# The second layer's normalised rows: scaled by ScalarE and VectorE and turned plainly, in place of products with a diagonal

## What is computed

```python
def second_block(x, ...):
    h = rms_norm(x, norm_mix_pre)
    u = h @ w_in                       # queries, keys, values, gates, convolution parts
    ... attention and a short convolution give y ...
    x = x + rms_norm(y @ w_out, norm_mix_post)
    h = rms_norm(x, norm_ffn_pre)
    gu = causal_dwconv(h @ w_ffn_up, ffn_conv_w)
    g, up = split(gu)
    y = (gelu(g) * up) @ w_ffn_down
    return x + rms_norm(y, norm_ffn_post)
```

## Time and profile before

| | |
|---|---|
| median of 3 runs | 1407.34 us (1405.52 to 1411.5) |
| the profiled execution | 1411.11 us, span 1409.3 us |
| granted TensorE clock, mean | 0.984 of full |
| TensorE busy | 1335.4 us (95% of the span) |
| VectorE busy | 757.2 us (54%) |
| ScalarE busy | 579.9 us (41%) |
| GpSimd busy | 456.9 us (32%) |
| chain that ended last | TensorE 76%, VectorE 15%, ScalarE 3% |

### The profile page before, as it was taken

One profiled execution on the slowest core, in us unless ns is written; L12 is line 12 of the kernel. 1 busy time (PEld: TensorE's weight loads), 2 busy tenths in 40 slices (PEclk: granted clock), 3 DMA queues, 4 the chain that ended last, 5 costly groups with the idle time before them and its releaser, 6 DMA issues.

```text
span 1409.3 us, 22598 instructions
## 1 busy us (share of the span) xinstructions
PE 1335.4 (95%) x9338; PEld 1111.0 (79%) x9338; DVE 757.2 (54%) x1246; ACT 579.9 (41%) x879; POOL 456.9 (32%) x131
## 2 busy tenths in 40 slices
PE   4999888889999999999999999999999999999998
PEld 3778677777788888888888787777798888888886
DVE  7788688664765444354327538787265444443002
ACT  7535465253442223221126545655265334433212
POOL 4424243033214434444422320000213433443344
PEclk8999899998999999999999999999999999999999
DMA  9564400302323333223313511101212232223211
GB/s 377 219 235 165 149 3 2 122 25 69 101 79 120 125 145 120 90 90 125 114 63 104 230 61 34 58 31 61 105 60 90 93 115 92 90 90 126 98 60 60
DMA packets 25901, 147.92 MB, mean 105 GB/s; under 512 B 2849, under 2 KB 4001, under 8 KB 11209
## 3 DMA queue, kind: packets, MB, share of 16 engines
q1 hardware_dynamic: 22272, 134.21, 26.6%
q10 hardware_dynamic: 3528, 12.28, 2.3%
HBM read 144.36 MB, written 4.74 MB: 106 GB/s over the span
## 4 chain that ended last, share of the span: by engine, by line
PE 76%; DVE 15%; ACT 3%; issue 2%; DMA 2%; POOL 1%; SPq 0%; DVEq 0%; ACTq 0%; POOLq 0%
PE bank L2198 22%; PE bank L2199 21%; PE bank L2200 21%; PE bank L2466 4%; DMA raw<-in_weights 2%; DVE xres L1760 1%; DVE raw L1812 1%; PE bank L1204 1%; ACT weight_hi L1409 1%; PE bank L1197 1%; DVE xres L1763 1%; PE bank L1188 1%; POOL weight_lo L1355 1%; POOL xres L1390 1%; DVE bank L1756 1%
## 5 line engine op out<-in xcount | busy, mean ns | idle before, releaser
L1355 POOL TENSOR_TENSOR weight_lo<-raw,weight_hi 128x2048 fp32r<-128x2048 f32 (+2 forms) x84 | 388.9, 4630 | 816.4 <-ACT weight_hi L1409 816.4
L2198 PE MATMUL bank<-act_hi,weight_hi 128*128 128x512 f32 (+1 forms) x1136 | 435.6, 383 | 18.3 <-DVE act_lo L1760 10.0
L2199 PE MATMUL bank<-act_lo,weight_hi 128*128 128x512 f32 (+1 forms) x1136 | 424.8, 374 | 0.0
L2200 PE MATMUL bank<-act_hi,weight_lo 128*128 128x512 f32 (+1 forms) x1136 | 424.7, 374 | 0.0
L1409 ACT ACTIVATE weight_hi<-raw 128x2048 fp32r<-128x2048 f32 (+1 forms) x98 | 185.3, 1891 | 428.9 <-PE bank L2200 394.7
L2198 PEld LDWEIGHTS bank<-act_hi,weight_hi 128*128 128x128 f32 x1136 | 215.2, 189 | 66.6 <-issue 18.3
L2200 PEld LDWEIGHTS bank<-act_hi,weight_lo 128*128 128x128 f32 x1136 | 215.1, 189 | 38.8
L2199 PEld LDWEIGHTS bank<-act_lo,weight_hi 128*128 128x128 f32 x1136 | 215.4, 190 | 34.6 <-issue 0.2
L2198 PE MATMUL bank<-weight_hi,hid_hi 128*128 128x512 f32 x352 | 136.9, 389 | 0.0
L2199 PE MATMUL bank<-weight_lo,hid_hi 128*128 128x512 f32 x352 | 136.9, 389 | 0.0
L2200 PE MATMUL bank<-weight_hi,hid_lo 128*128 128x512 f32 x352 | 136.9, 389 | 0.0
(11 more groups left out here) (385 smaller groups left out, 1826.2 us busy)
## 6 DMA issues: line engine op xcount, KB each, us to landing
raw<-in_weights SPq DMA_DIRECT2D x112, 1024.0 KB, 4.8
first_piece<-in_first_ada SPq DMA_DIRECT2D x15, 512.0 KB, 15.8
w<-in_w ACTq DMA_DIRECT2D x2, 2048.0 KB, 12.0
bias_rows<-bias_rows_once ACTq DMA_DIRECT2D x1, 2560.0 KB
xres<-in_x SPq DMA_DIRECT2D x4, 512.0 KB, 5.6
strip<-bias_rows ACTq DMA_DIRECT2D x1, 2048.0 KB, 8.3
out<-xres SPq DMA_DIRECT2D x3, 512.0 KB, 2.6
row_a<-in_ln_g ACTq DMA_DIRECT2D x2, 512.0 KB, 4.1
```

The costliest lines, as they stand in the source:

```text
L1355: pool.tensor_tensor(wlo[i % SPLIT][:, :size], raw[n % RAW][:, :size], whi[i % SPLIT][:, :size], ALU.subtract).then_inc(lo_ready, 1)
L2198: pe.matmul(o, l[0], r[0], start=first, stop=False)
L2199: pe.matmul(o, l[0], r[1], start=False, stop=False)
L2200: return pe.matmul(o, l[1], r[0], start=False, stop=last)
```

## The change

The diagonal and its tile are gone. The row itself is scaled into `xn2`, and `turn_half` turns it with `pe.transpose` as in the first layer. ScalarE scales rows 0 and 2 whole (1024 wide) and the second half of row 3, and in h4 that of row 1; VectorE, behind its reciprocal in `inverse_x`, scales the first half of row 3, in h4 the first half of row 1, and in h3 both halves of row 1, each 512 wide. Two semaphores, `rows_act` and `rows_vector`, take the place of `xn3_ready`, and `turn_half` waits for a row's parts where their blocks begin (`scaled_rows_of`). In h4, row 0 is turned before the k = 0 step of the last row of `out2_3` and row 1 between it and the k = 1 step; and row 0 is scaled ahead of the conversion and not behind it.

```diff
-    diag, _ = place("diag", [P, TT, P], F32, arena + 6 * TT * DM)

...
- ... "ss3", "root3", "xn3_ready", "grow_ready", ...
+ ... "ss3", "root3", "rows_act", "rows_vector", "grow_ready", ...
...
@@ -714,6 +713,12 @@
     row2_a, a2 = place("row2_a", [P, DM], F32, e1 - FT * SEQ * 4)
     row2_b, a2 = place("row2_b", [P, DM], F32, a2)
 
+
+    def scaled_rows_of(e):
+
+        act, vector = S["rows_act"], S["rows_vector"]
+        return ([[(act, 1)], [(vector, 1), (vector, 2)], [(act, 2)], [(vector, 3), (act, 3)]],
+                [[(act, 4)], [(vector, 4), (act, 5)], [(act, 6)], [(vector, 5), (act, 7)]])[e]
 
     def second_act(act, a, convert, affine_half, square_x, root_x, scaled_x):
         act.wait_ge(load["strip0"], 16)
@@ -848,9 +853,9 @@
                 squares_of_rows("mix2", 0, x, rms_t)
             square_x(1, t)
             root_x(1, t)
+            scaled_x(1, t)
             if half == 0:
                 convert()
-            scaled_x(1, t)
             square_x(1, u)
             root_x(1, u)
             scaled_x(1, u)
@@ -1152,7 +1157,7 @@
                 mm = pe.transpose(bank(("turn_v", name))[:, n * t:n * t + n], before_turn[name][0:n, tok(t)], ident[0:n, 0:n])
             fill(("turn_v", name), mm)
 
-        dense_halves(FIRST_UNITS[:2], "h3", xres, (S["xn3_ready"], 0))
+        dense_halves(FIRST_UNITS[:2], "h3", xn2, scaled_rows_of(0))
         for n, name in enumerate(FIRST_UNITS):
             if name == "gates":
                 gates_features()
@@ -1232,8 +1237,8 @@
         dense_rows("mix2", "out2", 4, [(act_hi, act_lo)] * 2 + [(out_hi, out_lo)] * 2,
                    ready={0: (S["y2_lo"], 2), 1: (S["y2_lo"], 4), 2: drained_at(("values", PAIR_END[1]), "dve"),
                           3: drained_at(("values", PAIR_END[3]), "dve")}, turned=True,
-                   turn=("h4", xres, (S["xn3_ready"], TT)))
-        dense_halves(("up2_0", "up2_1"), "h4", xres, (S["xn3_ready"], TT))
+                   turn=("h4", xn2, scaled_rows_of(1)))
+        dense_halves(("up2_0", "up2_1"), "h4", xn2, scaled_rows_of(1))
         for m in range(2, FT):
             dense_feature(f"up2_{m}", 2)
         dense_rows("ff2", "down2", FT // 2, [(hid_hi, hid_lo)] * (FT // 2),
@@ -1728,8 +1733,9 @@
 
         def scaled_x(e, t):
 
+            h = slice(SEQ * (t % 2), DM)
             act.wait_ge(S["x_inverse"], TT * e + t + 1)
-            a.done(act.activation(diag[:, t, :], ident[:], ACT.Copy, scale=x_sums[:, t:t + 1]), S["xn3_ready"])
+            a.done(act.activation(xn2[:, t, h], xres[:, t, h], ACT.Copy, scale=x_sums[:, t:t + 1]), S["rows_act"])
 
         for half in range(2):
             t, u = 2 * half, 2 * half + 1
@@ -1740,7 +1746,8 @@
             for x in (t, u):
                 square_x(0, x)
                 root_x(0, x)
-                scaled_x(0, x)
+                if x != 1:
+                    scaled_x(0, x)
             if half == 0:
                 convert()
             affine_half("h3", half, "nmp")
@@ -2100,6 +2107,9 @@
         def inverse_x(e, t):
             dve.wait_ge(S["x_rms_root"], TT * e + t + 1)
             d.step(V.reciprocal(x_sums[:, t:t + 1], x_sums[:, t:t + 1]), S["x_inverse"])
+            for j in range(2 if (e, t) == (0, 1) else t % 2):
+                h = slice(SEQ * j, SEQ * j + SEQ)
+                ts(xn2[:, t, h], xres[:, t, h], x_sums[:, t:t + 1], sem=S["rows_vector"])
 
         def affine_lo_half(stage, half, part):
 
@@ -2296,26 +2306,28 @@
                     if ready is not None and n in ready:
                         pe.wait_ge(*ready[n])
                 for t in tiles:
-                    if turn is not None and (n, t) == (n_units - 1, TT - 1):
-                        turn_half(turn[0], 0, *turn[1:])
                     for k in range(2):
+                        if turn is not None and (n, t) == (n_units - 1, TT - 1):
+                            if turn[0] == "h4":
+                                turn_half(turn[0], 0, *turn[1:], rows=(k,))
+                            elif k == 0:
+                                turn_half(turn[0], 0, *turn[1:])
                         mm = rows_product(stage, n, n_units, last_two[n], parts, t, k, turned)
                 if tiles == middle and n == n_units - 2:
                     mm.then_inc(unit_used, 1)
 
-        def turn_half(stage, half, source, ready):
-
-            for i in range(KC // 2):
-                claim(pe, (stage, half, i))
-            for t in range(2):
-                pe.wait_ge(ready[0], ready[1] + 2 * half + t + 1)
+        def turn_half(stage, half, source, ready, rows=(0, 1)):
+
+            for t in rows:
+                if t == 0:
+                    for i in range(KC // 2):
+                        claim(pe, (stage, half, i))
+                parts = ready[2 * half + t]
                 for k in range(KC):
+                    if k % (KC // len(parts)) == 0:
+                        pe.wait_ge(*parts[k * len(parts) // KC])
                     at, x = HALF * (k % 2) + P * t, source[:, 2 * half + t, P * k:P * k + P]
-                    o = bank((stage, half, k // 2))[:, at:at + P]
-                    if stage == "h2":
-                        mm = pe.transpose(o, x, ident[:])
-                    else:
-                        mm = pe.matmul(o, x, diag[:, 2 * half + t, :], start=True, stop=True)
+                    mm = pe.transpose(bank((stage, half, k // 2))[:, at:at + P], x, ident[:])
                     if t and k % 2:
                         fill((stage, half, k // 2), mm)
 
@@ -2676,8 +2688,8 @@
                 out1(*args)
 
         dense_rows("mix1", "out1", 4, [(act_hi, act_lo)] * 4, begun, {2: (S["y_lo"], 2), 3: (S["y_lo_last"], 2)},
-                   turn=("h2", xres, (S["xn_ready"], TT)))
-        dense_halves(("up1_0", "up1_1"), "h2", xres, (S["xn_ready"], TT))
+                   turn=("h2", xres, [[(S["xn_ready"], TT + t + 1)] for t in range(TT)]))
+        dense_halves(("up1_0", "up1_1"), "h2", xres, [[(S["xn_ready"], TT + t + 1)] for t in range(TT)])
         for m in range(2, FT):
             dense_feature(f"up1_{m}", 2)
             if m == GATE_ROWS_AT:
```

More of the change, by code:

```diff
@@ L640, in build @@
                              "y_hi", "y_lo_first", "y_lo", "y_lo_last", "gates_ready", "var1", "root1", "xn2_ready", "affine2", "hid_hi_ready",
-                             "hid_ready", "var2", "root2", "offset_ready", "ss3", "root3", "xn3_ready", "grow_ready", "strip_ready", "blk_ready", "hc_ready", "low_ready",
+                             "hid_ready", "var2", "root2", "offset_ready", "ss3", "root3", "rows_act", "rows_vector", "grow_ready", "strip_ready", "blk_ready", "hc_ready", "low_ready",
                              "zeroed", "cmp_scaled", "exp_done", "gate_ready", "o_ready", "upper_free", "y2_hi", "y2_lo", "squares_ready",
```

## The result

The changed kernel takes 1411.58 us against 1408.44 us before, medians of 20 runs each; the ratio is 1.0025 with a 95% interval of 1.0015 to 1.0035, so 3.5 us (2.1 to 4.9) slower; the medians themselves differ by 3.1 us. The forecast was 2.0 us slower and 1409.3 us. Of the 2.3 us by which the time lies over that, 1.1 come from its base, the median of three runs (1407.34) in place of twenty, and the rest from the change.

What follows compares the result with a forecast made beforehand. TensorE was taken as full nearly everywhere, with VectorE late in h3 and h4's second half. Losses of 0.9 us in h3 and 1.1 in h4 sum to 2.0 on 1407.34, giving 1409.3 us; range 1405.3 to 1413.5.

Steps and rivals of the forecast that it cites:

- TensorE's saving: Plain turns in h3 and h4 save TensorE 7.7 us over eight rows, most of it hidden behind waits.
- rival C: h4's VectorE multiplication is not held by GpSimd: h4 1.1 us shorter, kernel 1407.1 us; chance 0.12.
- VectorE's multiplications in h3: Two for row 1 delay h3's first product by 1.04 us; h3 loses 0.9 us in all.
- The side sum with 1.03 us for one multiplication: Upper bound per multiplication: h3 loses 1.3 us, h4 is 0.8 us worse, kernel 1411.4 us.
- The multiplication held by GpSimd: In h4's first half, row 1's multiplication waits for GpSimd's split, ending 2.9 us later than its work needs.
- The claim of up2_0's banks: In h4, up2_0 waits for four low parts: it starts 1.6 us later, or 0.7 earlier without GpSimd.
- The chain through ScalarE's conversion to row 3: In h4's second half, the late conversion shifts VectorE up to row 3's reciprocal by 1.25 us; first product +1.1 us.
- rival B: TensorE's clock falls in the new gaps of h3 and h4: all together 4.3 us, 1413.6 us; chance 0.15.
- the first layer's row: Evidence against a clock fall: in the first layer's second half, turns with 1.6 us idle kept the clock at 1.00.
- the fall at 988 us: Evidence for a clock fall: after thin work the clock stood at 0.50, then 0.69, a loss of 1.6 us.
- D: TensorE's time counts everywhere in h3 and h4: 7.7 us saved, 1399.6 us; chance 0.03.
- E: GpSimd also holds h3's multiplications, costing up to 4.6 us more, 1413.9 us; chance 0.05.

Runs made afterwards that it cites:

- best, first form: Changed kernel with h3's rows 0 and 1 back to the diagonal and h4's row 1 scaled wholly by ScalarE; ratio to the kernel before 1.0002.
- the best form of both: Changed kernel with all of h3 back to the diagonal and h4's row 1 scaled wholly by ScalarE; ratio to the kernel before 1.0009.

## Why the prediction was right, and where it was short

**TensorE's saving.** Right that it is worth next to nothing. The instructions fell from 128 to 64 and nothing of the 7.7 us arrived, since in three of the four halves TensorE waits anyway, and in the fourth the held multiplication puts off row 1. Without that one (h4's row 1 by ScalarE) h4 is 1.13 us shorter than before, and rival C had worked out 1.1. Two runs put a price on the view that a shorter turn can't harm: it lengthens the idle time, and with it (best, first form) came a fall of the clock that neither the diagonal's longer turns nor the turns issued twice had.

**VectorE's multiplications in h3.** Right: 1.01 us for two, the first product +1.05 (forecast 1.04), and h3 0.88 to 0.90 over before in the four traces where the clock fell late, by the work behind it (forecast 0.9). The side sum with 1.03 us for one multiplication was off: it counts 2.5 of them in h3, where three stand in VectorE's way (1.5 us and not 1.3). Nothing hangs on it, since one took 0.49 us.

**The multiplication held by GpSimd.** Right, and shown: 3.32 us for 512 columns, 3.12 for 128, both ending with the split, and h4 2.83 us shorter without it. The rule of the Trainium skill, "SBUF — State Buffer", section "Who interferes with whom", held at both widths. The claim of up2_0's banks was right too: without the hold it starts 25.36 us behind the anchor, 0.38 earlier than before; the forecast for such a case was 0.7. With the clock up, TensorE's idle time before up2_0 is there as forecast (1.33 us with 128 columns, forecast 1.2). In the run without the hold the fourth low part ends at 1030.32 + 4 x 0.515 = 1032.38 and the product starts at 1032.73; these 0.35 us between were left out. Rival C (not held) is out; its price for h4, 1.1 us under before, is what h4 shows once VectorE has no part in row 1.

**The chain through ScalarE's conversion to row 3.** Right where the clock stays up: with 128 columns h4 is 0.82 us over before.

**The clock, rival B.** This is what the forecast had wrong: it was put beside the sum, with a chance of 0.15, and it happened in both first halves. The fall came in h4's stall in every trace in which VectorE was held for 512 columns with TensorE waiting two microseconds behind it (the changed kernel and four others), and in h3's first half in every trace with the multiplications there and the idle time unfilled. Its price was small because, as the working had it, slack hides most of it in h3: 0 or 0.55 us by when it falls (44.22 or 44.78); in h4 it is 0.6 over the forecast's 1.1. Together 1.15 us, which makes the forecast's 2.0 the 3.15 of the trace. Rival B's own prices for the two first halves, 0.1 and 1.0, come to nearly the same sum, but by luck: the one was too low for this trace and the other too high. And as the 0.55 stands in one of five traces, 2.6 us is the likelier sum of the two stages; both lie inside the timing's 2.1 to 4.9. The step that failed is the reading of the earlier trace rows: the first layer's row, 1.00 with 1.6 us idle, was taken as the nearer case for idle times of 3.1 and 2.1 us, when the fall at 988 us stood beside it. Taken over all fourteen traces the two rows look less alike: the first layer's has 1.00 in every one, while the fall near 987 us is in nine of them. So one trace can't give the chance of a fall in a gap, and only a few stand behind the comparisons here (1.82 us of idle time without a fall in h4 is one trace, 2.0 us with a fall are five). What the Trainium skill, "TensorE: Matmul & The Clock Gate", "Part 4: PE-mode transpose", says of turns and the clock, that they don't count as busy for it as products do, is not borne out here: with turns alone, 0.66 and 0.21 us idle, it stayed at 1.00.

**Rivals D and E.** D is out with TensorE's waits. E didn't happen: GpSimd's next split began at 744.51, and the multiplications were done at 743.94.

**Open.** Why timing finds the best form of both at 1.0009 when its two stages are 1.1 us shorter. The scatter outside the stages (6.8 us in where the anchor of h3 lies, 2.3 us between the stages) is larger than the effect. A good part of the answer lies in the clock: over its 11 timed executions the granted clock is 0.9864 in the mean, over the 15 of the kernel before 0.9891. A fall between the stages, 3.4 us at 0.50, takes 0.0012 off that mean and costs some 0.75 us, so the difference is worth about 1.7 us, an estimate, of the 2.4 between stages and timing. The first form of the best (0.9846 against 0.9876) and h4's row 1 by ScalarE (0.9842 against 0.9874) stand lower too; h3 by the diagonal doesn't (0.9880 against 0.9874). Only one execution of each kernel was traced, so where those falls lie, and whether the edit brings them, stays open.

## What to carry to other kernels

Work that is moved off a full engine is worth nothing where that engine waits, and costs where it lands: look first at who is late in the stage. Before a VectorE operation out of SBUF is put somewhere, look at what GpSimd does at that moment; the same half row cost 0.49 us in one place and 3.32 in the other. And price a new idle time on TensorE twice, once as itself and once with the slower clock behind it, less the slack before the next wait.

## What the runs showed of the hardware

A shorter turn can be the slower one: rows 2 and 3 of h3 turned once left the clock at 0.50 behind them (two traces), turned twice (one trace), or by the diagonal, at 1.00, and the work behind the stage came 1.1 us earlier with twice the instructions. The fall doesn't start at a fixed point of the idle time: with the same instructions and the same 3.10 us idle it was there at 746 to 748 us in the changed kernel (0.58), and in other traces only behind the first products, which decided over 0.56 us. Between the stages, near 987 us, the clock fell in nine of fourteen traces of the same instructions, and each fall there made the stretch some 0.75 us longer. And a 128-column multiplication waited as long for GpSimd as one of 512.
